# The delta-rule loop of a two-layer block: shared tiles of unsolved rows, a compact state, one product for key and query scores, and another order of the outputs

## The reference, cut to what matters

```
v_new = u_i - w_i @ state
o_i   = q_i @ state + a_i @ v_new
state = state * gl + k_i^T @ v_new
```

## Time and profile before

| | us |
|---|---|
| median of three runs | 2690.39 |
| span of the profiled execution | 2685.3 |
| PE busy | 2583.9 (96%) |
| VectorE busy | 1817.1 (68%) |
| ScalarE busy | 926.3 (34%) |
| POOL busy | 549.2 (20%) |

### The profile page before, as it was taken

One profiled execution on the slowest core, in us unless ns is written; L12 is line 12 of the kernel. 1 busy time (PEld: TensorE's weight loads), 2 busy tenths in 40 slices (PEclk: granted clock), 3 DMA queues, 4 the chain that ended last, 5 costly groups with the idle time before them and its releaser, 6 DMA issues. The chain is left out here.

```text
span 2685.3 us, 35832 instructions
## 1 busy us (share of the span) xinstructions
PE 2583.9 (96%) x14026; PEld 2060.8 (77%) x14026; DVE 1817.1 (68%) x2735; ACT 926.3 (34%) x1610; POOL 549.2 (20%) x265
## 2 busy tenths in 40 slices
PE   7999999999899999999999999999999999999998
PEld 5875558884478887788888888867997888887787
DVE  5894997772667668999773553333277666666987
ACT  4335454420444545333332222232233223232432
POOL 1212544430000004333201222134400000003330
PEclk9999999999999999999999999999999999999999
DMA  4011032230133336333221222243413222225231
GB/s 162 32 64 67 32 126 96 90 133 24 55 114 118 103 118 223 111 110 126 91 82 53 78 70 75 81 166 108 145 55 88 79 87 79 87 79 214 100 126 63
DMA packets 192759, 262.24 MB, mean 98 GB/s; under 512 B 15952, under 2 KB 121808, under 8 KB 192208
## 3 DMA queue, kind: packets, MB, share of 16 engines
q1 hardware_dynamic: 192592, 259.95, 28.6%
HBM read 196.80 MB, written 61.93 MB: 96 GB/s over the span
## 5 line engine op out<-in xcount | busy, mean ns | idle before, releaser
L1381 PE MATMUL ps<-gl_t,gl_slot 128*128 128x512 f32 x1056 | 244.6, 391 | 2.4 <-DVE gl_t L3986 2.4
L1389 PE MATMUL ps<-b_hi,a_hi 128*128 128x512 f32 x592 | 231.6, 391 | 9.5 <-DVE sb L3630 7.6
L1381 PEld LDWEIGHTS ps<-gl_t,gl_slot 128*128 128x128 f32 x1056 | 199.3, 189 | 44.6 <-DVE gl_t L3986 3.1
L2756 POOL TENSOR_TENSOR s_raw<-ff_raw 128x1024 f32<-128x1024 f32 x2 | 5.1, 2545 | 962.6 <-DMA ff_raw<-hid_rows 513.6
L3630 DVE TENSOR_TENSOR sb<-sb,ps 128x512 f32<-128x512 f32 x272 | 173.5, 680 | 33.3 <-PE ps L1389 33.2
L1381 PE MATMUL ps<-gl_b,gl_slot 128*128 128x512 f32 x768 | 182.1, 395 | 3.7 <-DVE gl_slot L4018 3.7
L1381 PE MATMUL ps<-ff_t,slot 128*128 128x512 f32 x768 | 179.2, 393 | 4.4 <-DVE ff_t L3284 4.4
L1381 PE MATMUL ps<-H_hi,tw_hi 128*128 128x512 f32 x448 | 175.6, 392 | 0.0
L1381 PE MATMUL ps<-H_rest,tw_hi 128*128 128x512 f32 x448 | 174.4, 389 | 0.0
L1381 PE MATMUL ps<-H_hi,tw_lo 128*128 128x512 f32 x448 | 174.3, 389 | 0.0
L1381 PEld LDWEIGHTS ps<-gl_b,gl_slot 128*128 128x128 f32 x768 | 146.4, 191 | 35.1 <-DVE gl_slot L4018 2.4
(11 more groups left out here) (475 smaller groups left out, 6053.9 us busy)
## 6 DMA issues: line engine op xcount, KB each, us to landing
wraw<-in_w_ff SPq DMA_DIRECT2D x16, 1024.0 KB, 5.9
ff_raw<-ff_rows SPq DMA_DIRECT2D x8, 2048.0 KB, 7.9
slab_raw<-in_w_ff SPq DMA_DIRECT2D x16, 1024.0 KB, 5.1
ff_rows<-quad SPq DMA_DIRECT2D x61, 256.0 KB, 2.0
traw<-in_w_in SPq DMA_DIRECT2D x28, 512.0 KB, 4.3
wq_raw<-in_w_in SPq DMA_DIRECT2D x6, 2048.0 KB, 8.5
wraw<-in_w_gate SPq DMA_DIRECT2D x22, 512.0 KB, 3.9
wraw<-in_w_up SPq DMA_DIRECT2D x22, 512.0 KB, 5.1
```

The costliest lines, as they stand in the source:

```text
L1381: mm = nc.tensor.matmul(out_ap, stationary(a, k), moving(c, k), start=(k == 0 and n == 0), stop=(k == kts - 1 and n == 2))
L1389: mm = nc.tensor.matmul(out_ap, stationary(a, k), moving(c, k), start=(fresh and k == 0 and n == 0), stop=(k == 1 and n == 2), skip_group_ ...
L2756: G.tensor_tensor(s1, s3, a22, ALU.add).then_inc(dn_as, 1)
```

## The change

- *Shared tiles.* `Xw` goes. The value half of `KVt[i % 2][c]` is the tile of unsolved rows `X_of(i, c)`: tile c = 0 holds rows 0 to 63 of direction 0 and rows 64 to 127 of direction 1, that is what steps 0 and 1 solve; tile 1 holds the rest. `forward(i, s)` makes both directions in one bank; steps 1 and 2 take 64 stationary columns per direction (K = 128), step 3 takes 32 rows and 32 columns. `less_forward` is one subtraction of 128 rows.
- *Compact state.* `Sc[d]` is 128 x 4 x 64 and holds no zeros. The products with it have 64 rows. The decay of the keys is now in `KdT`, made by POOL in `decayed_queries`.
- *Scores.* Keys and queries lie beside each other in `KQ`; one product has 256 moving columns, and `weights[b][d]` takes both. E is multiplied in by `weighted(i, d, part, x)`.
- *Order.* Outputs are split in `carried_outputs` and `own_outputs` by odd and even heads.
- *Loads.* Six transfers per round instead of two; `wout` is split, and its first four row blocks are loaded after the last solve.

The diff, cut to its core. Its last part is the order of one round on VectorE:

```diff
 def gdn_order():
+        order += [("kS", i, c, x) for c in both for x in both] if i > 0 else []
+        order += pair("y", 0) + ([("kq", 0, d, x) for d in both for x in both] if i == 0 else [])
+        order += behind(i - 1, 0) + [("w", i, 1)] + pair("y", 1) + [("w", i, 2)]
+        order += ahead(0, 0) + pair("y", 2) + (ahead(0, 1) if more else behind(i, 0))
+        order += [("w", i, 3)] + behind(i - 1, 1) + pair("y", 3) + ahead(1, 0)
+        order += ([("kv", i, d) for d in both] + ahead(1, 1)) if more else behind(i, 1)
...
             def kv_load(i):
                 if i >= 2:
-                    sp.wait_ge(gdn_X, 2 * (i - 1))
+                    solved(sp, i - 2)
...
+            def scores(i, d, part):
+                for j in both:
+                    for x in both:
+                        q = 2 * part + j
+                        keys_and_queries = KQ[HD * x:HD * x + HD, :, q, t * P:(t + 1) * P]
...
+            def carried(i, c):
+                for q in range(4):
+                    for x in both:
+                        for r in both:
+                            d = c if r == 0 else 1 - c
+                            part = slice(HD * r, HD * r + HD)
+                            mm = nc.tensor.matmul(ps[part, banks[x], q * HD:(q + 1) * HD], half(KdT[d], 2 * q + x)[:, part],
+                                                  half(Sc[d][i % 2], 2 * q + x), start=True, stop=True)
...
+            def forward(i, s):
+                for h in range(HEADS):
+                    for d in both:
+                        rows = block_rows(d, 3) if s == 3 else slice(HD, P) if (s == 2) != (d == 1) else slice(0, HD)
+                        seen = block_rows(d, 2) if s == 3 else slice(0, P)
+                        mm = nc.tensor.matmul(ps[rows, b, h * HD:(h + 1) * HD], weights[i % 2][d][seen, h, 0, rows],
+                                              yv[i % 2][d][seen, h * HD:(h + 1) * HD], start=True, stop=True)
...
             def update(i, d):
                 for q in range(4):
-                    cols = slice(q * P, (q + 1) * P)
-                    mm = nc.tensor.matmul(ps[:, b, cols], Kdec[d][:, cols], yv[i % 2][d][:, cols], start=True, stop=True)
+                    for x in both:
+                        cols = slice((2 * q + x) * HD, (2 * q + x + 1) * HD)
+                        mm = nc.tensor.matmul(ps[x * HD:(x + 1) * HD, b, q * HD:(q + 1) * HD], Kdec[d][:, cols],
+                                              yv[i % 2][d][:, cols], start=True, stop=True)
...
+            def carried_outputs(i, d):
+                for q in range(4):
+                    for x in both:
+                        nc.tensor.matmul(ps[:, banks[x], q * HD:(q + 1) * HD], half(QdT[(i + 2) % 3][d], 2 * q + x),
+                                         half(Sc[d][i % 2], 2 * q + x), start=(q == 0), stop=False, skip_group_check=True)
...
+            def own_outputs(i, d, x):
+                for q in range(4):
+                    h = 2 * q + x
+                    mm = nc.tensor.matmul(ps[:, b, q * HD:(q + 1) * HD], weights[i % 2][d][:, h, 1, :],
+                                          yv[i % 2][d][:, h * HD:(h + 1) * HD], start=(i == 0),
+                                          stop=(i == 0 or q == 3), skip_group_check=True)
...
                 solve(i, 0)
+                    carried_outputs(i - 1, 0)
+                forward(i, 1)
+                    own_outputs(i - 1, 0, 0)
                 solve(i, 1)
+                    own_outputs(i - 1, 0, 1)
+                forward(i, 2)
+                scores(i + 1, 0, 0)
                 solve(i, 2)
+                scores(i + 1, 0, 1)
+                forward(i, 3)
+                    carried_outputs(i - 1, 1)
+                    own_outputs(i - 1, 1, 0)
                 solve(i, 3)
+                    own_outputs(i - 1, 1, 1)
+                scores(i + 1, 1, 0)
                     for d in both:
                         update(i, d)
+                scores(i + 1, 1, 1)
...
             def decay_args(i):
                     if i > 0:
-                        wait_drained(pool, G_GDN, GDN_AT[("kq", i - 1, d, 1)])
+                        query_weights_ready(pool, i - 1, d)
...
             def decayed_queries(i):
+                    if i > 0:
+                        G.tensor_tensor(KdT[d], QdT[(i + 2) % 3][d], KTall[:, :, t * P:(t + 1) * P], ALU.mult
+                                        ).then_inc(gdn_keys, 1)
...
+            def weighted(i, d, part, x):
+                heads = slice(4 * part + x, 4 * part + 4, 2)
+                V.tensor_tensor(weights[i % 2][d][:, heads, :, :], ps[:, b, :].rearrange("p (h n c) -> p h n c", h=2, n=2),
+                                E[d][:, heads, :].unsqueeze(2).broadcast_to([P, 2, 2, P]), ALU.mult).then_inc(drained[b], 1)
...
+            def less_carried(i, c):
+                for x in both:
+                    b = arrived("kS", i, c, x)
+                    V.tensor_tensor(rest[:, x::2, :], rest[:, x::2, :], heads_of(ps[:, b, 0:256], HD), ALU.subtract
+                                    ).then_inc(drained[b], 1)
...
+            def less_forward(i, s):
+                rest = X_of(i, s // 2)
+                V.tensor_tensor(rest, rest, ps[:, b, :], ALU.subtract).then_inc(drained[b], 1)
...
                 if i > 0:
-                    less_carried(i)
+                    less_carried(i, 0)
+                    less_carried(i, 1)
                 second_drain(i, 0)
+                less_forward(i, 1)
+                collect(i - 1, 0)
+                second_drain(i, 1)
+                collect(i - 1, 1)
                     state_decay(i, 0)
+                less_forward(i, 2)
+                weighted(i + 1, 0, 0, 0)
                 second_drain(i, 2)
+                weighted(i + 1, 0, 0, 1)
+                weighted(i + 1, 0, 1, 0)
+                less_forward(i, 3)
+                weighted(i + 1, 0, 1, 1)
+                collect(i - 1, 2)
                 second_drain(i, 3)
+                    state_decay(i, 1)
+                collect(i - 1, 3)
+                weighted(i + 1, 1, 0, 0)
                     state_add(i)
+                weighted(i + 1, 1, 0, 1)
+                weighted(i + 1, 1, 1, 0)
+                weighted(i + 1, 1, 1, 1)
```

More of the change, by code:

```diff
@@ L108, in gdn_order, with ahead, behind @@
         more = i + 1 < NT
-        def ahead(name, d):
-            return [(name, i + 1, d, x) for x in both] if more else []
         def pair(name, s):
             return [(name, i, d, s) for d in both]
[L116 to L128, removed]
+        def ahead(d, part):
+            return [("sc", i + 1, d, part, x) for x in both] if more else []
+        def behind(j, d):
+            return [("o", j, 2 * d + x) for x in both] if j >= 0 else []
+        order += [("kS", i, c, x) for c in both for x in both] if i > 0 else []
[4 more added lines that the diff above has]
+        order += ([("kv", i, d) for d in both] + ahead(1, 1)) if more else behind(i, 1)
     return {key: n for n, key in enumerate(order)}
@@ L1601, in solve @@
+            def solve(i, s):
+                if s == 0 and i == 0:
+                    pe.wait_ge(kv_in[0], KV_LOADS)
+                if s == 0 and i > 0:
+                    for x in both:
+                        ready("kS", i, 0, x)
+                if s == 2 and i > 0:
+                    for x in both:
+                        ready("kS", i, 1, x)
+                if s > 0:
+                    ready("w", i, s)
+                banks = [bank("y", i, d, s) for d in both]
                 for h in range(HEADS):
@@ L1653, in _ @@
             for d in both:
-                scores("kk", 0, d)
+                first_scores("kk", d)
             for k in range(8):
@@ L1659, in _ @@
                 if i > 0:
-                    for d in both:
-                        carried(i, d)
-                outputs(i - 1, 0, 1)
+                    for c in both:
+                        carried(i, c)
                 solve(i, 0)
@@ L2715, in _ @@
             wait_full(pool, *front("Z", 7))
-            pool.wait_ge(kv_in[0], 32)
-            for d in both:
-                G.tensor_copy(Xw[d], KVt[0][d][:, GW:2 * GW]).then_inc(gdn_X, 1)
             clear(0)
@@ L3149, in _ @@
             dve.wait_ge(c_out, 32)
-            for d in both:
-                ins = V.memset(Sbd[d][1].rearrange("p a b -> p (a b)"), 0.0)
-            ins.then_inc(gdn_S0, 1)
-            dve.wait_ge(gdn_S0, 1)
             for t in range(1, NT, 2):
```

282 lines of the change are left out of this document (138 added, 144 removed).

## The result

The changed kernel takes **2743.32 us** (median of 4 runs, 2738.87 to 2744.08), the kernel before 2690.33 (4 runs, 2687.57 to 2694.24). The ratio is 1.0192, with a 95% interval of 1.0178 to 1.0207: slower by 53 us, where 2682 was forecast. The time is far above the range, 2662 to 2703. The profiled execution, from which all rows of the changed kernel come, is the fastest of the four.

The account below looks back on a forecast made before the run. Bound: PE's own work and, close to it, the chain through VectorE. Gains of 2.1 (rounds 0, 1), -0.4 (rounds 2 to 5), 2.4 (round 6 to 7), 0.95 and 3.0 (round 7), together 8.1 us, gave 2682; range 2662 to 2703.

Parts of the forecast that it names:

- The mechanism of the stop: Rounds 1 to 6: direction 1's late exponentials delay ScalarE's copy behind the first solve by 2.8 us.
- 32 alternating records of 128x64: Block products of steps 1 and 2, and the update: taken as 1.0 us each, upper end 1.87.
- round without the late copy: A full steady round at full clock if ScalarE didn't stand in the way: 21.0 us, 3.6 less than before.
- round with it, PE not standing (e3): A round with ScalarE's copy late, before any clock loss: 23.55 us, 1.1 less than before.
- stop at the first block product: PE stands still 2.55 us in each of rounds 1 to 6, waiting for ScalarE's copy.
- Round 7 and the tail behind its last solve: Last round: solve 3 comes 0.95 us sooner after the first product; VectorE's queue behind it ends 3.0 us sooner.
- G: Start of a round's first block product: 2.05 us after the first solve, 4.6 with the late copy.
- 1.2 us per stop: Price of low PE clock after each stop in rounds 1 to 6: 1.2 us, between 0 and 3.4.
- The second: Rival: clock falls at each stop and stays down 6.8 us, 13 us more in all, 2695; chance 0.1.
- The first: Rival: weight loads of two column groups don't overlap, products cost 1.87 us, 18 us more in all, 2700; chance 0.24.
- The third: Rival: late exponentials don't bind, 2.55 + 1.2 us less in six rounds, 2660; chance 0.1.
- The fourth: Rival: a round doesn't change, as a step is half a microsecond short everywhere, 2690; chance 0.06.

Follow-up runs that it names:

- e3: Changed kernel with 7 unread products (17 in round 1) filling PE's stop before the first block product of rounds 1 to 6; 2692.17 us.
- e1: Changed kernel with ScalarE's eight direction 1 exponentials moved behind its step 1 copy in the next round; 2678.95 us.
- e10: e6 with direction 0's round 2 exponentials behind round 1's first copy, and unread products in round 0's stops and before first solves; not told apart from e6.
- e12: Kernel before, with ScalarE's copy of step 0 made six times in rounds 1 to 6, so PE stops at the first block product; 2720.75 us.
- e5: Changed kernel, stop kept, with block products and update ordered so neighbouring products use the same half of the columns; 2723.77 us.
- e11: Changed kernel, stop kept, with only the block products ordered by direction; the update still alternates; 2726.16 us.
- e4: e1 with block products ordered by direction and the update by odd and even heads, so neighbours share a column group; 2692.77 us.
- e6: e1 with VectorE's first carried subtraction ahead of its last two weights and the second behind the copy of step 0; 2659.65 us.
- e2: Kernel before, with POOL's direction 1 addition also waiting for the next round's carried part of direction 1; 2709.4 us.

## Why the prediction was wrong

**The mechanism of the stop was right.** It said that ScalarE's exponentials for direction 1, two rounds on, would hold the copy behind the first solve, since POOL's addition has to wait for VectorE's last weights. In e3, where the clock doesn't blur it, the third solve starts at 546.56. VectorE's and POOL's rows, and ScalarE's:

```profile
551.21 2.07 DVE L3162 TENSOR_TENSOR sb<-ps,sb 128x512 f32<-128x512 f32 x3
...
553.45 2.36 POOL L2807 TENSOR_TENSOR sb<-sb 128x1024 f32<-128x1024 f32 x1 [1.85 <-DVE sb L3162]
...
555.84 2.44 ACT L2275 ACTIVATE sb<-sb 128x128 f32<-128x128 f32 x8 [1.76 <-POOL sb L2807]
558.31 0.57 ACT L2313 COPY sb<-ps 32x512 f32<-32x512 f32 x1
```

The weights end 6.7 us after that solve (forecast 6.7), the exponentials 11.7 (forecast 11.6).

**The steps at full clock** (forecast, then measured by starts, in e1 where not said otherwise):

```
32 alternating records of 128x64            1.0    1.08
one shared tile of the carried part         1.0    0.57 (64 records for both: 1.13, in e10)
8 records of 128x128, own outputs           0.94   1.03
first solve to first block product          2.05   2.14
first block product to solve 1              2.2    2.12
solve 1 to solve 2                          4.1    4.40
solve 2 to solve 3                          4.95   5.17
solve 3 to the next first solve             7.7    7.47
round without the late copy                21.0   21.30
round with it, PE not standing (e3)        23.55  24.22
stop at the first block product             2.55   2.93 to 3.23 (changed kernel, rounds 2 to 6)
```

None is off by more than 0.7 us. What the prediction counted per round, 24.63 before against 23.55 after, would have been 24.22: 0.4 us of gain instead of 1.1, over four rounds 2.7 us. Round 7 and the tail behind its last solve gained 0.8 and 3.9 us where 0.95 and 3.0 were forecast. The first product of round 2 came 4.1 us later than forecast. Round 1 is the round for which the sum names no price of the clock, and its stop is the longest. PE's timeline:

```profile
429.10 1.98 PE L1682 MATMUL ps<-sb 128*64 128x64 f32 x32 [8.02 <-issue]
```

Here the exponentials of both directions (423.08 to 427.87) stand ahead of the copy (427.89), since POOL's additions for them start only at 420.71, released by a transfer of the row decays. Behind the stop some 10 us are at 1.2 GHz. So of the 60 us between the forecast and the measured place of the product that needs the whole loop (609.6 and 669.68), 52 arose in rounds 2 to 5, 4.1 before and 4.5 in round 6, less 0.8 at the end; the excess in each of these rounds is clock, but for 0.7 us a round.

**The failing step** is one sentence: "As PE is the bound after G, low clock costs half its time; I take 1.2 us per stop, between 0 and 3.4." Its rule is nearly right and its size wrong by a factor of more than eleven: measured 13.8 us per round. The same sixteen groups of products, from the first block product to the last scores, in the changed kernel and in e3:

```profile
457.20:487.77 30.57, 30.57 (x304) 0.50 0.21 70
...
535.09:551.82 16.73, 16.73 (x306) 1.00 0.35 117
```

The difference is 13.84 us, all that a round loses to the clock. At half the clock the groups take 1.83 times as long, not twice, so low clock costs 45% of its time and not 50. Nothing comes back through shorter waits: PE waits 1.0 us for VectorE before the next first solve in either case. The length of the low stretch, 31 to 34 us where 3.4 to 6.8 were read, is what was wrong. In rounds 2 to 5 the clock makes 4 x 13.8 = 55.3 us, the shorter round takes back 4 x (24.63 - 24.22) = 1.6: 53.7, measured 52.7. The low time in the loop gives an upper end from another side: 160.4 - 20.4 = 140 us more than before, at 45% some 63, of which some was idle time that the clock doesn't touch.

The 1.2 came from the stops of the earlier trace rows, followed by 3.4 to 6.8 us of low clock. Those rows were read rightly, but for products that the change removes: behind them stood, besides solves and scores, 128x128 and 128x32 stationaries. e12 gives the old products such a stop in each of six rounds, and its profiled run has 3.4 to 10.2 us behind four of them and none behind two; e5 and e11 have the changed kernel's stop and block products by direction, and 3.4 to 13.7 us. A price read from rows holds for what stands in those rows, and the part of the change that made PE faster also changed how long it stays slow.

**The rivals.** The second ("stays down 6.8 us", 2695) was right in kind and far too small. The first is refuted (1.08 us, not 1.87), but not by the reason given against it. In the earlier trace rows, L1618 takes 0.053 us a record where L1604, with as many moving columns, takes 0.032, and L1618's neighbours are the eight heads of one direction, all in one column group. That is close to e4's 0.056 for neighbours in the same half, so this row showed no load hidden under a product and, if anything, spoke for the rival. The 1.0 was right because the change alternates. The third is what e1 makes of the kernel, and its 2660 is e6's time; e1's own is 2679, as its clock falls without the stop too. The fourth is refuted. Of what the prediction named as signs against itself, one came: a PE clock of 1.2 GHz over more than 4 us in each round.

**What stays open.** Why the clock stays at 1.2 GHz while the profile has PE busy in 30.35 of 31.00 us. Busy time in the profile is evidently not what decides (the ends of PE's records are modelled, so a busy PE need not be a full one); the block products have to do with it (e11) and are not all of it, since solves, scores and outputs are there in e11 too, and e12's stop, besides other products, is 0.7 us shorter. And why 1.2 GHz so often ends at the round's scores and carried part. No run measured these products by themselves, and none filled a stop with something other than dense products, so what exactly makes the clock fall or hold is not shown.

## What to carry to other kernels

A stop of PE is priced by what PE does after it, at the clock which that leaves: read the clock behind stops in the kernel that is changed only if the products behind them stay the same, and otherwise take the whole next stretch at half speed as the far end of the range. Where an in-order engine feeds PE (here ScalarE, with eight exponentials ahead of a copy that PE waits for), look for the work that can go behind that copy: moving one call took 64 us off. A stop that can't be removed can be filled: products that nobody reads (3.3 us in a round, more in round 1) were worth 51 us.

## What the runs showed of the hardware

- PE can be busy by the profile throughout and stay at 1.2 GHz: 30.57 of 30.57 us in the changed kernel (0.50), 30.78 of 30.80 in e1 (0.50), 21.98 of 22.00 in e10 (0.53). TensorE: Matmul & The Clock Gate (the Trainium skill, section Part 1, What's actually happening) says that activity releases the throttle. Here activity as the profile shows it did not, for 30 us at a time.
- The clock fell within 2 us behind a wait of 1.0 us (e1 at 488.63, e10 at 554.17), in one round of many alike; behind a stop of 2.47 us it did not (e12 at 515.90).
- The same sixteen groups took 30.57 us at 1.2 GHz and 16.73 at 2.4 (the changed kernel, e3): 1.83 times, not twice.
- 128x64 stationaries that alternate between the column halves, all in the same rows, cost 0.034 us a record, and 0.056 in e4 where neighbours have the same half. TensorE: Matmul & The Clock Gate (the Trainium skill, section Part 3, The mechanism) lets loads overlap only when the row groups differ; by it both orders would cost the same. The measurement decides: neighbours in different column groups overlap too, be it their loads or their products.
- Two VectorE operations with both inputs in SBUF took 3.43 us beside POOL's addition of 2.66 (e2), and a single one between 0.68 and 2.84. GPSIMD Engine Reference (the Trainium skill, section 1. Specifications) names contention between GpSimd and such VectorE instructions; this run agrees.
